# The head of a two-block transformer kernel: the first two modulations on VectorE instead of TensorE, three chunks taken along step by step instead of two

## The chip, the cores and the metric

The kernel runs on one core of a Trainium2 chip, as one launch. The metric is the device time of that core in microseconds (us), lower is better. The median of three runs of the kernel before is 1721.9 us (1711.86 to 1724.2).

## The reference

256 tokens of width 1024 go through two blocks in fp32. The first block mixes a gated linear recurrence and a stick-breaking attention and has a gated feed-forward part; the second has two attentions and a mixture of 32 experts. The change touches the first lines of the first block alone:

```python
mod = c @ ada_w[l] + ada_b[l]                       # c: 1 x 1024, ada_w: 1024 x 6144
sh1, sc1, gt1, sh2, sc2, gt2 = [m[:, None, :] for m in jnp.split(mod, 6, axis=-1)]
h = rmsnorm(x, norm1_g[l]) * (1.0 + sc1) + sh1      # x: 256 x 1024
p = h @ w_in[l]                                     # w_in: 1024 x 7168
xr, yr, q, k, v, ga, gb = jnp.split(p, cuts, axis=-1)
...
q = head_rmsnorm(q.reshape(b_, s_, ATT_HEADS, HEAD_DIM), q_norm_g[l])
k = head_rmsnorm(k.reshape(b_, s_, ATT_HEADS, HEAD_DIM), k_norm_g[l])
```

## The kernel before, in words

Activations lie transposed: `xT` and `hT` are 128 partitions x 8 blocks x 256 tokens, where block k holds the features 128k to 128k+127. Each engine has a program written out by hand, and the order in it is the order of the code; the engines wait for one another through counting semaphores. Weights come as pieces of 1 MB through a ring of 17 slots (`ring`). One list, `plan`, sets the order of the pieces; SyncE issues them in that order, and from the 18th on it waits until the piece that lay in the slot has been used. After the plan's pieces the 384 pieces of the experts' weights go through the same ring.

The head of the program works so. ScalarE squares `xT` in four pieces (L1190). VectorE adds the four to one (L1635, L1637), and TensorE sums the 128 partitions with a matrix of ones in one matmul of 256 columns (L529). ScalarE takes the root (L1172), VectorE the reciprocal (L1596), and eight multiplications (L1652) make `hT` out of `xT`. The shift sh1 and the scale sc1 come block by block: a piece `("ada", 0, n)` holds the 2 x 128 columns of `ada_w` for block n. TensorE multiplies it by c in eight narrow matmuls (`shift_and_scale`, L537), ScalarE copies four partial rows out of PSUM (L1202), TensorE sums and turns them (`shift_and_scale_turn`, L548), VectorE adds the bias and makes the gain (L1657, L1659), and ScalarE applies both to block n of `hT` (L1206). As soon as block k of `hT` is there, `first_chunks` (L561) adds its share to the first two chunks of q, ("qk", 0) and ("qk", 1): four matmuls of 256 columns per k, into banks 0 and 1. A chunk is 256 columns of `w_in`, 16 matmuls in all. These three kinds of work alternate on TensorE, one after the other, for n = 0 to 9.

Behind this each of the six other q and k chunks runs in one go (L515), with one matmul of 512 columns for a head norm between two chunks (`qk_norm`, L592). That needs VectorE's copy of the chunk (L1687) and ScalarE's square of it (L1214). The root (L1220), a reciprocal of 512 elements (L1692) and two scalings follow. VectorE also evaluates a softplus of `rg_lambda` in some 30 operations on 128 x 8, most of them between the steps of the head (L1640 to L1677), the rest after it.

The later modulations are summed on VectorE already: c lies broadcast over the partitions in `cb`, the weights are transposed, and two multiplications with an accumulating output (L1617) make 2 x 128 values of one piece.

Of the kernel before, what the change touches and what calls it, by code (L numbers as in the profile page):

```python
# [15 lines left out]
S = 256  # L16
# [17 lines left out]
def _layout_cols():  # L34
    n = 0
    for name, w in (("e4", 1), ("c", 8), ("ada_b", 48), ("b_ada2", 48), ("norm1", 8), ("norm2", 8),
                    ("conv_w", 32), ("conv_b", 8), ("ba", 8), ("bx", 8), ("lam", 8), ("qg", 1), ("kg", 1),
                    ("fw", 144), ("fb", 48), ("pre_mix", 8), ("post_mix", 8), ("pre_ffn", 8),
                    ("post_ffn", 8), ("gq", 2), ("gkv", 1)):
        COLS[name] = (n, w)  # L40
        n += w
    return n
# [63 lines left out]
piece_done ada_row ada_tr cb ada_use mod  # L106
qk_raw qk_sq qk_sum qk_rt qk
pad xp_cp xc vv gel
att_qk att_ln att_l1 att_cum att_lg att_p att_o att_y
# [32 lines left out]
class Board:  # L142
# [35 lines left out]
    def lay_scratch(self):  # L178
# [17 lines left out]
        self.lt = [carve(8) for _ in range(6)]  # L196
        self.sq1 = [carve(512) for _ in range(4)]
        self.rst1 = carve(256)
        self.rows = carve(512)
# [76 lines left out]
    def lay_pieces(self):  # L276
# [15 lines left out]
        ada(0, range(3, 8))  # L292
        for n in range(2, 8):
            w_in(("qk", n), (8, 12)[n // 4] + n % 4)
# [41 lines left out]
        ada0 = [("ada", 0, k) for k in range(8)]  # L336
        for key in ada0 + [key for key, _, _ in plan if key not in ada0]:
            if key[0] not in ("b1", "ada") or key[:2] == ("ada", 0):
# [88 lines left out]
def sync_program(e, K):  # L427
# [4 lines left out]
    for i, (key, src, n) in enumerate(K.plan):  # L432
        if i >= RING:
# [66 lines left out]
def tensor_program(e, K):  # L500
# [29 lines left out]
    def shift_and_scale(n):  # L530

        v = landed(("ada", 0, n))
        if n >= 2:
            e.wait_ge(S.ada_row, n - 1)
        for k in range(8):
            g = 32 * (k % 4)
            ins = mm(B[5 + n % 2][g:g + 32, 0:256], K.C("c", k).to_broadcast([128, 32]), v[:, 256 * k:256 * k + 256],  # L537
                     start=(k < 4), stop=(k >= 4), skip_group_check=True)
        ins.then_inc(S.piece_done, 1)

    def shift_and_scale_turn(n):

        e.wait_ge(S.ada_row, n + 1)
        if n >= 2:
            e.wait_ge(S.hn, n - 1)
        for m in range(2):
            o = 256 * (n % 2) + 128 * m
            ins = mm(B[3 + n % 2][:, m:m + 1], K.rows[:, o:o + 128], K.C("e4"), start=True, stop=True,  # L548
                     skip_group_check=True)
        ins.then_inc(S.ada_tr, 1)  # L550

    def first_chunks(k):

        for c in range(2):
            v, b = K.piece(("qk", c)), K.main_bank(("qk", c))
            if k == 0:
                landed(("qk", c))
            if c == 0:
                e.wait_ge(S.h, k + 1)
            for j in range(2):  # L560
                ins = mm(b[:, 256 * j:256 * j + 256], v[:, k * 256 + j * 128:k * 256 + j * 128 + 128], K.hT[:, k, :],  # L561
                         start=(k == 0 and j == 0), stop=(k == 7), skip_group_check=True)
            if k == 7:
                ins.then_inc(S.piece_done, 1)
# [29 lines left out]
    for n in range(8):  # L594
        if n >= 2:
# [308 lines left out]
    e.wait_ge(S.consts, 4)  # L904
# [252 lines left out]
def scalar_program(e, K):  # L1157
    S, B, a, act = K.S, K.bank, K.a, e.activation
# [27 lines left out]
    e.wait_ge(S.consts, 3)  # L1186
# [10 lines left out]
    for n in range(9):  # L1197
        if n < 8:
            landed(("ada", 0, n))
            if n >= 2:  # L1200
                e.wait_ge(S.ada_tr, n - 1)
            act(K.rows[:, 256 * (n % 2):256 * (n % 2) + 256], B[5 + n % 2][:, 0:256], ACT.Copy).then_inc(S.ada_row, 1)  # L1202
        if n:
            k = n - 1
            e.wait_ge(S.hn, k + 1)
            act(K.hT[:, k, :], K.hT[:, k, :], ACT.Identity, bias=K.modc[:, 0, k:k + 1],  # L1206
                scale=K.mc[:, k:k + 1]).then_inc(S.h, 1)
# [377 lines left out]
def vector_program(e, K):  # L1585
# [40 lines left out]

    e.memset(K.eps[:, :], EPS).then_inc(S.consts, 1)
# [3 lines left out]
    for c in range(1, 4):  # L1631
        e.wait_ge(S.sq, c + 1)
        if c > 1:
            e.wait_ge(S.vec, done.n)
        tt_(K.sq1[0], K.sq1[0], K.sq1[c], ALU.add).then_inc(S.vec, done.one())  # L1635
    e.wait_ge(S.vec, done.n)
    tt_(K.sq1[0][:, 0:256], K.sq1[0][:, 0:256], K.sq1[0][:, 256:512], ALU.add).then_inc(S.vec, done.one())  # L1637
    lt = K.lt
    e.wait_ge(S.coef, 1)
    ts_(lt[1], lt[0], 2.0, None, ALU.add).then_inc(S.vec, done.one())  # L1640
    e.wait_ge(S.vec, done.n)
    e.reciprocal(lt[1], lt[1]).then_inc(S.vec, done.one())
    e.wait_ge(S.vec, done.n)
# [846 lines left out]
```

## Time and profile before

| | us |
|---|---|
| median of 3 runs | 1721.9 |
| lowest and highest run | 1711.86, 1724.2 |
| profiled execution, first to last instruction (span) | 1709.3 |
| TensorE busy in it | 1613.8 (94%) |
| VectorE busy | 587.9 (34%) |
| ScalarE busy | 352.9 (21%) |
| head: until the last matmul of the first two chunks | about 43.8 |

Of the profiled execution the span alone is known. The lowest run is 2.6 us above that span. A busy TensorE is not one at its peak, since the ends of pipelined matmuls are modelled. An fp32 matmul shows as two MATMUL records.

### The profile page before, as it was taken

What the parts mean: (1) busy time and instruction counts of PE and PEld (TensorE: products, weight loads), DVE (VectorE), ACT (ScalarE), POOL (GpSimd) and SP (SyncE); (2) the same over time, 40 slices, a digit from 0 to 9 for tenths busy, and PEclk for the clock granted to TensorE, in tenths of its full rate; (3) what the DMA queues carried; (4) which work ended last, traced back from release to release, by engine and by line L of the source; (5) the groups of instructions that cost most, each with busy time, mean ns of one, the idle gap of its engine ahead of it and who ended that gap; (6) DMA issues with size and microseconds to landing.
All of it is one profiled execution on the core that took longest, in us unless ns stands there. A gap on an engine that the chain in (4) does not pass through costs nothing. (4 is left out here: it accounts for less than half of the span.)

```text
span 1709.3 us, 20875 instructions
## 1 busy us (share of the span) xinstructions
PE 1613.8 (94%) x7480; PEld 899.7 (53%) x7480; DVE 587.9 (34%) x1355; ACT 352.9 (21%) x658; POOL 0.2 (0%) x4
## 2 busy tenths in 40 slices
PE   7999989999999898879999998999999899999997
PEld 4888878788888776733333332333333233333332
DVE  3657762789710364232122111112112111212112
ACT  3126552332200134121111111111111110101111
POOL 0000000000000000000000000000000000000000
PEclk9999999999999998988999999999999899999999
DMA  9936675458963330238999999999999999999995
GB/s 396 395 133 246 246 274 183 160 202 324 386 250 120 127 131 1 99 127 361 420 420 420 421 419 420 421 420 420 419 421 420 420 414 405 420 420 420 420 420 224
DMA packets 77221, 545.49 MB, mean 319 GB/s; under 512 B 8944, under 2 KB 9456, under 8 KB 11536
## 3 DMA queue, kind: packets, MB, share of 16 engines
q1 hardware_dynamic: 76048, 542.31, 78.5%
q8 instruction: 94, 1.54, 0.4%
q10 hardware_dynamic: 1024, 1.18, 0.2%
q14 instruction: 55, 0.45, 0.1%
HBM read 542.41 MB, written 1.05 MB: 318 GB/s over the span
## 5 line engine op out<-in xcount | busy, mean ns | idle before, releaser
L1000 PE MATMUL bank<-ring,scr 128*64 128x512 f32 x2048 | 455.5, 600 | 10.5 <-DMA ring<-in_w_mlp 10.5
L515 PE MATMUL bank<-hT,ring 128*128 128x256 f32 x1664 | 369.7, 383 | 7.2 <-ACT hT L1180 7.2
L515 PEld LDWEIGHTS bank<-hT,ring 128*128 128x128 f32 x1664 | 319.6, 193 | 55.4 <-issue 11.6
L1000 PEld LDWEIGHTS bank<-ring,scr 128*64 128x64 f32 x2048 | 145.2, 138 | 303.5 <-issue 267.6
L1033 PE MATMUL bank<-ring,hT 128*64 128x512 f32 x1024 | 233.9, 597 | 1.9 <-DMA ring<-in_w_mlp 1.8
L2273 DVE TENSOR_SCALAR scr<-bank 128x256 f32<-128x256 f32 x64 | 27.0, 422 | 388.3 <-PE bank L1000 388.3
L1033 PEld LDWEIGHTS bank<-ring,hT 128*64 128x64 f32 x1024 | 68.4, 136 | 140.8 <-issue 131.7
L2343 DVE COPY hT<-bank 64x512 f32<-64x512 f32 x32 | 22.2, 694 | 313.4 <-PE bank L1033 283.8
L1500 ACT ACTIVATE scr<-scr 128x256 f32<-128x256 f32 x64 | 26.7, 417 | 494.8 <-DVE scr L2273 494.8
L1617 DVE SCALAR_TENSOR_TENSOR ring<-ring,cb 128x1024 f32<-128x1024 f32 x80 | 94.5, 1219 | 0.0
L713 PE MATMUL bank<-scr,ring 128*128 128x256 f32 x384 | 83.5, 379 | 1.6 <-ACT scr L1343 1.6
L713 PEld LDWEIGHTS bank<-scr,ring 128*128 128x128 f32 x384 | 72.9, 190 | 11.9 <-ACT scr L1343 2.0
L927 PE MATMUL bank<-scr 128*64 128x512 f32 x272 | 67.6, 620 | 7.2 <-DVE scr L2243 4.6
L1534 ACT ACTIVATE hT<-bank 128x512 f32<-128x512 f32 x32 | 19.1, 598 | 221.3 <-PE bank L943 221.3
L1071 PE MATMUL bank<-hT,scr 128*128 128x512 f32 x128 | 59.2, 605 | 0.8 <-ACT hT L1550 0.8
L927 PEld LDWEIGHTS bank<-scr 128*64 128x64 f32 x272 | 19.5, 142 | 46.5 <-issue 38.0
L1071 PEld LDWEIGHTS bank<-hT,scr 128*128 128x128 f32 x128 | 23.0, 189 | 37.1 <-issue 35.4
L943 PEld LDWEIGHTS bank<-con,scr 128*128 128x128 f32 x136 | 14.9, 146 | 35.0 <-issue 26.5
L2231 DVE COPY scr<-bank 64x256 f32<-64x256 f32 x64 | 27.0, 422 | 13.0 <-PE bank L933 11.7
L1946 DVE SCALAR_TENSOR_TENSOR scr<-scr,col 128x256 f32<-128x256 f32 x48 | 23.1, 481 | 20.5 <-ACT scr L1343 20.2
L1692 DVE RECIPROCAL scr<-scr 128x512 f32<-128x512 f32 x8 | 26.8, 3352 | 9.6 <-ACT scr L1220 9.6
L1986 DVE SCALAR_TENSOR_TENSOR xT<-bank,modc,xT 128x256 f32<-128x256 f32 x8 | 3.5, 479 | 77.4 <-PE bank L713 77.4
(394 smaller groups left out, 1391.7 us busy)
## 6 DMA issues: line engine op xcount, KB each, us to landing
ring<-in_w_mlp SPq DMA_DIRECT2D x384, 1024.0 KB, 23.2
ring<-in_w_in SPq DMA_DIRECT2D x28, 1024.0 KB, 14.8
ring<-in_up SPq DMA_DIRECT2D x24, 1024.0 KB, 7.0
ring<-in_w_ada SPq DMA_DIRECT2D x24, 1024.0 KB, 6.9
ring<-in_ada_w SPq DMA_DIRECT2D x16, 1024.0 KB, 4.9
ring<-in_down SPq DMA_DIRECT2D x12, 1024.0 KB, 14.9
ring<-in_ada SPq DMA_DIRECT2D x8, 1024.0 KB, 18.6
ring<-in_w2in SPq DMA_DIRECT2D x6, 1024.0 KB, 9.8
```

The source lines that it names most:

```text
L515: ins = mm(b[:, 256 * j:256 * j + 256], v[:, k * 256 + j * 128:k * 256 + j * 128 + 128], rhs[:, k, :], start=(k == 0), stop=(k == 7))
L713: ins = mm(b[j][:, 0:256], v[:, k * 256 + j * 128:k * 256 + j * 128 + 128], K.ff[:, kk * 8 + k, :], start=(kk == 0 and k == 0), stop=(kk = ...
L927: ins = mm(B[3][64 * hf:64 * hf + 64, :], K.sel[c][:, tt, :], K.h4[:, tt, hf * 512:(hf + 1) * 512], start=(tt == 0), stop=(tt == 1), skip_ ...
L1000: ins = mm(HID[0][n][64 * hf:64 * hf + 64, :], K.xe[0][x % 2][:, xo:xo + 64], v[:, o0:o0 + 512], start=False, stop=(k == 7), skip_group_ch ...
L1033: ins = mm((K.down_bank(x), B[1])[c][g:g + 64, :], K.aT[c][x % 2][:, 128 * q + 64 * hf:128 * q + 64 * hf + 64], v[:, j * 1024 + oh * 512:j ...
L1071: ins = mm(OUT[tt][oh][:, :], K.pairT[p % 2][oh][:, tt * 128:(tt + 1) * 128], K.ypair[oh], start=False, stop=False, skip_group_check=True)
L1500: act(K.w2[:, sl], K.actb[0][:, sl], ACT.Sigmoid, scale=1.702).then_inc(S.m_sig, 1)
L1617: ins = stt(w, w, 1.0, K.cb[:, :], ALU.mult, ALU.mult, accum_out=K.modc[:, n // 3, m:m + 1])
L1692: e.reciprocal(rst, rst).then_inc(S.vec, done.one())
L1946: stt(w[:, m, :], u[:, m, 1:257], C("fw", 48 + n), w[:, m, :], ALU.mult, ALU.add).then_inc(S.vec, done.one())
L2231: ins = e.tensor_copy(K.pairT[x // 2 % 2][g ^ x % 2][rows, :], B[3][rows, 0:256])
L2273: ts_(w[:, sl], gate, 7.0, None, ALU.min).then_inc(S.m_glu, 1)
```

## The change

The pieces `("ada", 0, n)` hold transposed weights now. VectorE multiplies each half by the broadcast c and sums along it (`first_modulation`), 2 operations of 1024 elements per block. c comes as one row of 4 KB; TensorE spreads it over the partitions with two matmuls of 512 columns, and VectorE copies the result to `cb`; a load of 512 KB goes. ScalarE makes shift and gain from the sums with two tiny operations per block. TensorE's narrow matmuls and turns and ScalarE's row copies are gone. TensorE sums the squares itself, in eight matmuls of 256 columns instead of three and a half additions on VectorE and one matmul. Three chunks go along step by step. The softplus moves behind the q and k chunks 3 to 6.

```diff
-        ada(0, range(3, 8))
-        for n in range(2, 8):
+        ada(0, [3])
+        w_in(("qk", 2), 10)
+        ada(0, range(4, 8))
+        for n in range(3, 8):
             w_in(("qk", n), (8, 12)[n // 4] + n % 4)
...
+            elif before[0] == "ada":
+                e.wait_ge(S.ada_sum, 2 * before[2] + 2)
...
         if key == ("ada", 0, 7):
-            e.dma_start(K.cb[:, :], a["cb"]).then_inc(S.ld_cb, 16)
             e.dma_start(K.con[:, 256:NCONST], a["consts"][:, 256:NCONST]).then_inc(S.ld_con2, 16)
...
+    e.wait_ge(S.ld_cb, 16)
+    e.wait_ge(S.consts, 1)
+    for n in range(2):
+        ins = mm(B[5 + n][:, :], K.one_row, K.c_row[:, 512 * n:512 * n + 512], start=True, stop=True)
+    ins.then_inc(S.c_mm, 1)
     e.wait_ge(S.ld_col, 32)
-    e.wait_ge(S.vec, 4)
-    mm(B[7][:, 0:256], ones, K.sq1[0][:, 0:256], start=True, stop=True).then_inc(S.nsum, 4)
...
-    for n in range(10):
-        if n < 8:
-            shift_and_scale(n)
-        if 1 <= n < 9:
-            shift_and_scale_turn(n - 1)
-        if n >= 2:
-            first_chunks(n - 2)
+    for c in range(4):
+        norm_sum(0, c, K.sq1[c])
...
+    def first_step(c, k):
+
+        v, b = K.piece(("qk", c)), K.main_bank(("qk", c))
+        for j in range(2):
+            ins = mm(b[:, 256 * j:256 * j + 256], v[:, k * 256 + j * 128:k * 256 + j * 128 + 128], K.hT[:, k, :],
+                     start=(k == 0 and j == 0), stop=(k == 7), skip_group_check=True)
+        if k == 7:
+            ins.then_inc(S.piece_done, 1)
...
     for n in range(8):
-        if n >= 2:
+        if n >= 3:
             chunk(("qk", n))
         if n:
             qk_norm(n - 1)
...
+    e.dma_start(K.c_row, a["c_row"]).then_inc(S.ld_cb, 16)
     e.dma_start(K.con[:, 0:256], a["consts"][:, 0:256]).then_inc(S.ld_col, 16)
     e.dma_start(K.col[:, :], a["cols"]).then_inc(S.ld_col, 16)
...
-    for n in range(9):
-        if n < 8:
-            landed(("ada", 0, n))
-            if n >= 2:
-                e.wait_ge(S.ada_tr, n - 1)
-            act(K.rows[:, 256 * (n % 2):256 * (n % 2) + 256], B[5 + n % 2][:, 0:256], ACT.Copy).then_inc(S.ada_row, 1)
...
+    e.wait_ge(S.gain, 1)
+    for k in range(8):
+        e.wait_ge(S.ada_sum, 2 * k + 1)
+        act(K.mc[:, 8 + k:9 + k], K.modc[:, 0, k:k + 1], ACT.Identity, bias=C("ada_b", k)).then_inc(S.act, done.one())
+        e.wait_ge(S.ada_sum, 2 * k + 2)
+        act(K.mc[:, k:k + 1], K.modc[:, 0, 8 + k:9 + k], ACT.Identity, bias=K.mc[:, 16 + k:17 + k],
+            scale=C("norm1", k)).then_inc(S.act, done.one())
+        e.wait_ge(S.hn, k + 1)
+        e.wait_ge(S.act, done.n)
+        act(K.hT[:, k, :], K.hT[:, k, :], ACT.Identity, bias=K.mc[:, 8 + k:9 + k],
+            scale=K.mc[:, k:k + 1]).then_inc(S.h, 1)
...
+    def first_modulation(k):
+
+        i = K.at[("ada", 0, k)]
+        v = K.piece(("ada", 0, k))
+        e.wait_ge(S.ring[i % RING], 16 * (i // RING + 1))
+        for j in range(2):
+            m, w = 8 * j + k, v[:, 1024 * j:1024 * j + 1024]
+            ins = stt(w, w, 1.0, K.cb[:, :], ALU.mult, ALU.mult, accum_out=K.modc[:, 0, m:m + 1])
+            ins.then_inc(S.ada_sum, 1)
...
+        if n == 4:
+            softplus_first()
+        elif 4 < n < 7:
+            softplus_terms(4 * n - 20, 4 * n - 16)
+        elif n == 7:
+            softplus_last()
```

On TensorE the steps of the head stood like this before. L537 is the product with c of one piece, L548 the turn, L561 the first two chunks, L592 the norm of a head; w0, w1, ... are the slots' semaphores.

```order
L529 MATMUL bank7<-scr,con 128x256 [waits vec,ld_col]
L537 MATMUL bank5<-ring,col 32x256 [waits w0]
...
L561 MATMUL bank0<-hT,ring 128x256 [waits h,w2]
L561 MATMUL bank0<-hT,ring 128x256
L561 MATMUL bank1<-hT,ring 128x256 [waits w4]
L561 MATMUL bank1<-hT,ring 128x256
L537 MATMUL bank6<-ring,col 32x256 [waits ada_row,w5]
L537 MATMUL bank6<-ring,col 32x256 x7
L548 MATMUL bank3<-col,scr 128x1 [waits hn,ada_row]
```

Now it is the following, where L532 spreads c, L525 and L526 sum the squares and L542 is a step of a chunk.

```order
L532 MATMUL bank5<-scr 128x512 [waits consts,ld_cb]
L532 MATMUL bank6<-scr 128x512
L525 MATMUL bank7<-scr,con 128x256 [waits sq,ld_col]
L526 MATMUL bank7<-scr,con 128x256
...
L542 MATMUL bank0<-hT,ring 128x256 [waits h,w2]
...
L542 MATMUL bank1<-hT,ring 128x256 [waits w4]
L542 MATMUL bank1<-hT,ring 128x256 x3
...
L542 MATMUL bank2<-hT,ring 128x256 [waits w6]
L542 MATMUL bank2<-hT,ring 128x256 x7
...
L542 MATMUL bank2<-hT,ring 128x256 x2
L584 MATMUL bank<-scr,con 128x512 [waits qk_sq,ld_con2]
L584 MATMUL bank<-scr,con 128x512 [waits qk_sq]
```

Between two waits for `h` nothing but chunk matmuls is left; the third chunk catches up on k = 0 to 3 in a row of eight, and the norms of the first two heads' chunks stand behind one another.

On VectorE the head reads so now. L1627 fills `cb`, L1629 makes a term of the gains, L1638 is `first_modulation`, L1589 the reciprocal, L1643 the scaled blocks, L1695 the copy of a chunk.

```order
L1627 COPY cb<-bank5 128x512 [waits c_mm]
L1629 SCALAR_TENSOR_TENSOR mc<-col 128x8 [waits ld_col]
L1638 SCALAR_TENSOR_TENSOR ring,modc<-ring,cb 128x1024 [waits w0,vec]
L1638 SCALAR_TENSOR_TENSOR ring,modc<-ring,cb 128x1024
L1589 RECIPROCAL scr<-scr 128x256 [waits norm_rt]
L1643 TENSOR_TENSOR hT<-xT,scr 128x256 [waits rstd]
L1643 TENSOR_TENSOR hT<-xT,scr 128x256 x3
L1638 SCALAR_TENSOR_TENSOR ring,modc<-ring,cb 128x1024 [waits w1]
...
L1643 TENSOR_TENSOR hT<-xT,scr 128x256 x4
L1638 SCALAR_TENSOR_TENSOR ring,modc<-ring,cb 128x1024 [waits w3]
...
L1695 COPY scr<-bank0 128x512 [waits h,piece_done,ld_con2]
```

The eight pairs of products are one after another on VectorE, with the reciprocal and the eight scaled blocks between the first three of them.

## Rows read from the trace of the kernel before

**Rows 1.** The page: span, and TensorE and DMA in 40 equal slices.
```profile
span 1709.3 us, 20875 instructions
...
PE   7999989999999898879999998999999899999997
...
DMA  9936675458963330238999999999999999999995
```

**Rows 2.** Stretches: length, busy PE, PEld, DVE, ACT, POOL, granted clock, DMA share, GB/s.
```profile
12.00:14.00 2.00, 2.00 (x24) 0.96 (x20) 1.97 (x2) 0.38 (x1) 0.00 (x0) 1.00 1.01 422
...
42.70:85.50 42.80, 41.92 (x183) 34.35 (x182) 27.04 (x21) 7.78 (x13) 0.00 (x0) 1.00 0.97 395
...
811.90:854.60 42.70, 42.70 (x196) 14.46 (x192) 8.36 (x23) 4.54 (x9) 0.00 (x0) 1.00 1.01 420
```

**Rows 3.** The chain that ended last, two of its pieces: start, us, what.
```profile
1663.84 26.43 DMA ring<-in_w_mlp
1690.32 1.96 PE bank L1033 x8
```

**Rows 4.** What TensorE waited for after 43 us: total, times, longest.
```profile
PE bank L1000 <- DMA ring<-in_w_mlp: 10.5, 18, 1.3
PE bank L614 <- DVE scr L1735: 7.5, 4, 4.7
PE bank L515 <- ACT hT L1180: 7.2, 2, 3.6
```

**Rows 5.** Timeline of the head: start, us, engine, line, operation [idle before].
```profile
6.07 2.19 ACT L1190 ACTIVATE scr<-xT 128x512 f32<-128x512 f32 x4 [2.90 <-DMA xT<-in_xT]
...
9.30 0.21 ACT L1192 ACTIVATE scr<-col 128x8 f32<-128x8 f32 x1 [1.05 <-DMA col<-in_cols]
...
10.14 1.19 PE L529 MATMUL bank<-scr,con 128*128 128x256 f32 x2 [10.14 <-DVE scr L1640]
...
11.37 0.48 ACT L1172 ACTIVATE scr<-bank,eps 128x256 f32<-128x256 f32 x1
...
11.88 1.75 DVE L1596 RECIPROCAL scr<-scr 128x256 f32<-128x256 f32 x1 [0.96 <-ACT scr L1172]
...
13.67 2.77 DVE L1652 TENSOR_TENSOR hT<-xT,scr 128x256 f32<-128x256 f32 x8
...
16.63 1.93 PE L537 MATMUL bank<-ring,col 128*32 128x256 f32 x16 [0.78 <-DMA ring<-in_ada]
16.74 0.60 ACT L1206 ACTIVATE hT<-hT,modc,mc 128x256 f32<-128x256 f32 x1 [1.38 <-DVE mc L1659]
...
19.37 3.67 PE L561 MATMUL bank<-hT,ring 128*128 128x256 f32 x8
...
24.43 1.97 PE L561 MATMUL bank<-hT,ring 128*128 128x256 f32 x8
...
33.08 1.07 PE L537 MATMUL bank<-ring,col 128*32 128x256 f32 x16
...
34.08 0.61 PE L548 MATMUL bank<-col,scr 128*128 128x1 f32 x4
...
36.45 1.07 PE L537 MATMUL bank<-ring,col 128*32 128x256 f32 x16
```

**Rows 6.** Timeline behind the head: the norm of a head's chunk and full chunks.
```profile
43.17 1.35 DVE L1687 COPY scr<-bank 128x512 f32<-128x512 f32 x2 [1.32 <-PE bank L561]
...
43.90 1.29 ACT L1214 ACTIVATE scr<-scr 128x512 f32<-128x512 f32 x2 [2.64 <-DVE scr L1687]
...
44.67 1.10 PE L592 MATMUL bank<-scr,con 128*128 128x512 f32 x2 [0.88 <-ACT scr L1214]
...
45.60 7.07 PE L515 MATMUL bank<-hT,ring 128*128 128x256 f32 x32
...
52.51 1.02 PE L592 MATMUL bank<-scr,con 128*128 128x512 f32 x2
...
53.37 7.07 PE L515 MATMUL bank<-hT,ring 128*128 128x256 f32 x32
```

**Rows 7.** Timeline of VectorE: two sums of a later modulation; a k chunk.
```profile
126.80 1.22 DVE L1617 SCALAR_TENSOR_TENSOR ring<-ring,cb 128x1024 f32<-128x1024 f32 x1
...
127.94 1.22 DVE L1617 SCALAR_TENSOR_TENSOR ring<-ring,cb 128x1024 f32<-128x1024 f32 x1
...
83.77 0.69 DVE L1687 COPY scr<-bank 128x512 f32<-128x512 f32 x1 [1.60 <-PE bank L515]
```

**Rows 8.** Small operations of the head: groups by line, busy us, mean ns.
```profile
L1665 DVE TENSOR_SCALAR scr<-scr 128x8 f32<-128x8 f32 x8 | 1.4, 171 | 0.3
```

**Rows 9.** DMA issues: count, KB, us from issue to landing.
```profile
con<-in_consts ACTq DMA_DIRECT2D x1, 128.0 KB, 5.5
...
scr<-in_posc ACTq DMA_DIRECT2D x1, 1.0 KB, 1.8
```

More of the change, by code:

```diff
@@ L194, in carve_top @@
             return self.scr[:, place[1]:place[1] + n]
-        self.lt = [carve(8) for _ in range(6)]
+        self.lt = [self.modc[:, 1, 8 * n:8 * n + 8] for n in range(5)]
         self.sq1 = [carve(512) for _ in range(4)]
         self.rst1 = carve(256)
-        self.rows = carve(512)
+        self.c_row, self.one_row = carve(1024)[0:1], carve(128)[0:1]
         place[0] = 0
@@ L335, in lay_pieces @@
         self.done_at, n = {}, 0
-        ada0 = [("ada", 0, k) for k in range(8)]
-        for key in ada0 + [key for key, _, _ in plan if key not in ada0]:
-            if key[0] not in ("b1", "ada") or key[:2] == ("ada", 0):
+        for key, _, _ in plan:
+            if key[0] not in ("b1", "ada"):
                 n += 1
@@ L541, in shift_and_scale_turn @@
-    def shift_and_scale_turn(n):
-        e.wait_ge(S.ada_row, n + 1)
-        if n >= 2:
[L545 to L564, printed above, removed]
@@ L573, in tensor_program @@
+    landed(("qk", 0))
+    for k in range(2):
+        e.wait_ge(S.h, k + 1)
+        first_step(0, k)
+    landed(("qk", 1))
+    for k in range(2):
+        first_step(1, k)
+    for k in range(2, 4):
+        e.wait_ge(S.h, k + 1)
+        first_step(0, k)
+        first_step(1, k)
+    landed(("qk", 2))
+    for k in range(4):
+        first_step(2, k)
+    for k in range(4, 8):
+        e.wait_ge(S.h, k + 1)
+        for c in range(3):
+            first_step(c, k)
     e.wait_ge(S.ld_con2, 16)
@@ L1641, in vector_program @@
-    e.wait_ge(S.vec, done.n)
-    e.reciprocal(lt[1], lt[1]).then_inc(S.vec, done.one())
-    e.wait_ge(S.vec, done.n)
-    tt_(lt[1], lt[1], lt[0], ALU.mult).then_inc(S.vec, done.one())
-    e.wait_ge(S.vec, done.n)
-    tt_(lt[2], lt[1], lt[1], ALU.mult).then_inc(S.vec, done.one())
-    e.wait_ge(S.vec, done.n)
-    ts_(lt[3], lt[2], 1.0 / 19.0, 1.0 / 17.0, ALU.mult, ALU.add).then_inc(S.vec, done.one())
+    e.wait_ge(S.c_mm, 1)
+    for n in range(2):
+        e.tensor_copy(K.cb[:, 512 * n:512 * n + 512], B[5 + n][:, :]).then_inc(S.vec, done.one())
@@ L1649, in vector_program, with first_scaled @@
+    def first_scaled(k0, k1):
+        for k in range(k0, k1):
+            tt_(K.hT[:, k, :], K.xT[:, k, :], K.rst1, ALU.mult).then_inc(S.hn, 1)
+    e.wait_ge(S.vec, done.n)
+    first_modulation(0)
     norm_end(0, K.rst1)
     e.wait_ge(S.rstd, 1)
-    for k in range(8):
-        tt_(K.hT[:, k, :], K.xT[:, k, :], K.rst1, ALU.mult)
-    for n in range(8):
-        e.wait_ge(S.ada_tr, n + 1)
-        both = K.modc[:, 0, 0:16].rearrange("p (j b) -> p b j", j=2)[:, n, :]
-        bias = C("ada_b", 0, 16).rearrange("p (j b) -> p b j", j=2)[:, n, :]
-        tt_(both, B[3 + n % 2][:, 0:2], bias, ALU.add).then_inc(S.vec, done.one())
+    first_scaled(0, 4)
@@ L1658, in vector_program, with softplus_first @@
+    first_modulation(1)
+    first_scaled(4, 8)
+    for k in range(2, 8):
+        first_modulation(k)
+    e.sem_inc(S.mod, 1)
+    e.wait_ge(S.ld_con2, 16)
+    lt = K.lt
+    def softplus_first():
+        e.wait_ge(S.coef, 1)
+        ts_(lt[1], lt[0], 2.0, None, ALU.add).then_inc(S.vec, done.one())
         e.wait_ge(S.vec, done.n)
-        stt(K.mc[:, n:n + 1], K.modc[:, 0, 8 + n:9 + n], 1.0, C("norm1", n), ALU.add, ALU.mult).then_inc(S.hn, 1)
-        m = 15 - 2 * n
+        e.reciprocal(lt[1], lt[1]).then_inc(S.vec, done.one())
@@ new lines, in softplus_first, with softplus_terms, softplus_last @@
+        e.wait_ge(S.vec, done.n)
+        ts_(lt[3], lt[2], 1.0 / 19.0, 1.0 / 17.0, ALU.mult, ALU.add).then_inc(S.vec, done.one())
+    def softplus_terms(n0, n1):
+        for n in range(n0, n1):
+            e.wait_ge(S.vec, done.n)
+            tt_(lt[3], lt[3], lt[2], ALU.mult).then_inc(S.vec, done.one())
+            e.wait_ge(S.vec, done.n)
+            ts_(lt[3], lt[3], 1.0 / (15 - 2 * n), None, ALU.add).then_inc(S.vec, done.one())
+    def softplus_last():
+        e.wait_ge(S.vec, done.n)
+        stt(lt[3], lt[3], 2.0, lt[1], ALU.mult, ALU.mult).then_inc(S.vec, done.one())
+        ts_(lt[4], C("lam", 0, 8), -1.0, 0.0, ALU.mult, ALU.max).then_inc(S.vec, done.one())
+        e.wait_ge(S.vec, done.n)
+        tt_(lt[3], lt[3], lt[4], ALU.add).then_inc(S.vec, done.one())
+        e.wait_ge(S.vec, done.n)
+        ts_(K.sp8[:, 0:8], lt[3], 8.0, None, ALU.mult)
+        ts_(K.sp8[:, 8:16], lt[3], -8.0, None, ALU.mult)
+        ts_(K.hb[:, 0:8], C("ba", 0, 8), 0.5, None, ALU.mult)
+        ts_(K.hb[:, 8:16], C("bx", 0, 8), 0.5, None, ALU.mult).then_inc(S.gatec, 1)
```

67 lines of the change are left out of this document (15 added, 52 removed).

## The prediction

> **What bounds the kernel now.** I read the slices first, then stretches, then the end of the chain, then the timeline of the head. TensorE is busy nearly all along, and from the 20th slice to the last but one the DMA engines are full [rows 1]. In that stretch they move 420 GB/s beside a TensorE that is shown busy all the time [rows 2], and the chain's last long piece is 26.43 us of expert weights, with one piece's matmuls behind it [rows 3]. So the second half is paced by the stream of expert weights. That stream is no reason why a gain at the head should be lost: its slots are freed by TensorE's use of earlier pieces, so it starts earlier when TensorE gets there earlier. Nowhere in the kernel does an engine wait for a time, only for another engine. Between the head and the experts TensorE leads: its longest waits after the head are for VectorE and ScalarE, each some us in total [rows 4], and these engines wait for TensorE in turn. So what is won or lost until the head's end should reach the end of the kernel nearly whole.
>
> The question is then when TensorE starts the fourth q/k chunk, ("qk", 3). That is 53.37 us before [rows 6], behind the two chunks that go along, the norm of the first, the third chunk, and the norm of the second. In the head TensorE never rests: from 23 us a period is 3.37 us (36.45 - 33.08), which is product, turn and four chunk matmuls in line [rows 5]. Half of it is chunk work.
>
> **TensorE's clock.** The same eight records of L561 take 3.67 us at 19.37 us and 1.97 us at 24.43 us [rows 5]: the 1.2 and the 2.4 GHz level. The granted clock reads 1.00 even at 12 us [rows 2], so in this head the durations tell the level, not that column. TensorE had worked from 10.14 us on with narrow matmuls mostly and got to the higher level at about 23 us, when the first four full-width chunk matmuls were through. Per matmul of 256 columns I take 7.07 / 16 = 0.442 us at the higher level [rows 6] and at the lower (3.67 - 0.2) / 4 = 0.87 us [rows 5], where 0.2 is the tail that four of them show at the higher one, 1.97 - 4 x 0.442.
>
> **The change, part by part.**
> *c.* The row of c is 4 KB. Nothing of this size is loaded in the head; the nearest rows are 1.8 us for 1 KB in a quiet queue and 5.5 us for 128 KB beside the first loads [rows 9]. Issued at 0.74 us, it lands between 2.5 and 6.2 us; I take 3.5, near the small one. Two matmuls of 512 columns at the lower level are four of 256: 3.5 us, until 7.0 (6.0 to 9.7). Two copies of 0.68 us each [rows 6] end at 8.4 (7.4 to 11.1). The constants land at 9.3 us [rows 5], and 0.45 us later now behind one more issue, so VectorE starts its first products at about 9.9 (to 11.3) and ends them by 12.3 (to 13.7). The norm is not there before 17 us, so all of this is covered, by 3 us at the least. The Trainium skill, page "DMA: Bandwidth & Descriptors", section "Anatomy of one DMA — SWDGE (gpsimd) path", gives about 2 us of fixed cost per transfer; that would put the landing near 2.8 us, and the sum would not move.
>
> *The norm.* Before, one matmul at 10.14 us. Now eight, from 9.75 us on. At the lower level 8 x 0.87 = 7.0 us: end, with the tail's first tenth, at 16.85; at the higher level 3.5 us: 13.3. I take the lower, since before TensorE was at that level until 23 us. Root 0.48, reciprocal 1.75 [rows 5]: until 19.15, 5.5 us later than the 13.63 of before. Then blocks of 0.34 us: four until 20.55.
>
> *VectorE's sums.* Two per block, spaced 127.94 - 126.80 = 1.14 us [rows 7], so 2.3 us a block. The second block's: 20.55 to 22.85. Four more scaled blocks: 24.25. Six more pairs: 26.55, 28.85, and so on to 38.05. ScalarE adds 0.05 + 0.2 + 0.05 + 0.6 = 0.9 us, from a 0.21 us small operation and 0.60 us for a block [rows 5]. So block k of hT is ready at 20.2, 23.8, 27.5, 29.8, 32.1, 34.4, 36.7 and 39.0 us. The pieces are there: the fourth landed at 16.6 us [rows 5], and 1 MB at 422 GB/s [rows 2] is 2.5 us; in the new order the pieces for blocks 3 to 7 come sixth and eighth to eleventh, at 21.6, 26.6, 29.1, 31.6 and 34.1 us, each 2 us or more ahead of its sum.
>
> *TensorE's chunks.* The two matmuls of k = 0 run at 20.2. From 23.8 us 46 matmuls are left. I let the lower level hold for 3.6 us more (as long as the four of before took): 4.1 matmuls. The other 41.9 take 18.5 us: end at 45.9 us. Are blocks late in this? c0 and c1 reach k = 2 at 28.2 (ready 27.5), k = 3 at 30.0 (29.8); the third chunk's eight run until 35.3; then k = 4 to 7 start at 35.3, 38.0, 40.6, 43.3, all behind their blocks. So TensorE paces, not VectorE, and the end is 45.9.
>
> *Norms of the heads.* Chunk 0 is done 1.8 us before that; copy and square need 0.7 + 0.65 [rows 6], so its norm runs right at 45.9. Chunk 1 is done at 45.0; its square is ready at 46.5, and its norm follows the first. Two norms take 2 x 0.87. ("qk", 3) starts at 47.65 us, against 53.37: **5.7 us** earlier.
>
> *Softplus.* Some 30 small operations go to VectorE behind chunks 4 to 7. One is 0.17 us [rows 8], about 0.2 with its wait, so at most 8 x 0.2 = 1.6 us per chunk. VectorE idles 1.6 us there per k chunk [rows 7], and TensorE needs a copy only a chunk later: nothing. Without that cover it would be 1.6 us twice. What it frees in the head was idle time of VectorE. The 512 KB load that goes was not waited for.
>
> **Sum.** 1709.3 - 5.7 = 1703.6 us of span. As the lowest run is 2.6 us above the span shown and the median 12.6 above, I put the same difference on the median: 1721.9 - 5.7 = **1716.2 us**, -0.33%. Gain at the ends of the unknowns: without any lower level after 23.8 us, 1.8 more, 7.5; with the higher level from the norm on, blocks come 3.5 us earlier or, the last, when its piece allows (34.1 + 2.3 + 0.9 = 37.3 us), the third chunk has caught up at 31.6, and 31.6 + 4 x 2.65 = 42.2 is 3.7 earlier than 45.9: 9.4.
>
> **Rivals.**
> *The clock stays low (slower).* TensorE now rests from 16.85 to 20.2 and from 21.9 to 23.8 us, where before it did not. If the higher level does not come while it waits block by block, the 46 matmuls take 46 x 0.87 = 40.0 us, the end is 63.8, and ("qk", 3) starts at 65.6: 12.2 us slower, 1734.1. It decides at the point where the lower level has lasted 3.6 + 2 x 5.7 = 15 us, to 38.8 us. Against it: at the lower level four matmuls need 3.5 us and blocks come every 2.3, so TensorE has no gap at all from 23.8 us on, and before the level rose with just such work [rows 5]. The Trainium skill, page "TensorE: Matmul & The Clock Gate", section "What's actually happening", says that "the default state is throttled, and activity releases the throttle", and its section "HAM oscillation — how this bites in real kernels" that waits between short bursts of matmuls bring the low level back. By that rule the norm's matmuls buy nothing for the chunks, as in my sum; the trace of before agrees with the first sentence, and has no such gap to show the second.
> *VectorE paces.* If a sum takes longer beside 420 GB/s of writes than the 1.14 us of a quieter stretch, the last block is late. TensorE's last step is 2.65 us, so the last block has until 43.3 us: 4.3 us of slack over the 14 sums behind the norm, 0.31 us each. At 1.7 us a sum it would be 39.0 + 14 x 0.56 = 46.8, end 49.5, and the gain 2: 1720.
> *Won and lost again.* The 5.7 us turn into waits of TensorE for VectorE or ScalarE in the attention, whose chains are as long as before [rows 4]. VectorE's end of the q/k part is softplus plus copies later relative to TensorE. No change: 1721. Against it: in the q/k part both engines wait for TensorE [rows 6, 7].
> *More than said.* The higher level comes early: gain 7.5 to 9.4, 1712.5 to 1714.4.
>
> **How the numbers follow.** The forecast (gain 4 to 7.5) has 0.55, more than said 0.12, VectorE's pace 0.08, won and lost again 0.15, the low clock 0.10, of which most is a partial one. All of these lie within 1% of 1721.9, which is 17.2 us and about what a measurement of this kernel can tell from no change. The whole spread of cases, 1712.5 to 1734, is less wide than that. What may carry a result over the line is the spread of runs: 12.3 us between three of the same kernel. A median of the changed kernel that falls on the lowest run's side is 1711.9 - 5.7 = 1706; on the other side 1724.2 - 2 = 1722. I take 1704 to 1724. Faster by over 1%: 0.07; within 1%: 0.91; slower by over 1%: 0.02.
>
> **What would show it.** The first chunk matmuls of k = 1 near 24 us and TensorE without gaps behind them; the last of chunk 2 at about 46; L584 twice in a row; the first matmul of ("qk", 3) near 47.7 us; pairs of L1638 every 2.3 us without a wait for the ring from 24 to 38 us; the reciprocal L1589 near 17.4 us; the experts' full DMA stretch some 6 us earlier, at the same 420 GB/s. I am wrong if TensorE waits for h behind 30 us, if L542 stays at 0.87 us per matmul, if the row of c lands after 9 us, or if the stretch between ("qk", 3) and the experts gets longer.

## The result and the profile after

The changed kernel takes 1724.06 us (median of 20 runs, 1721.74 to 1725.87), the kernel before 1712.9 us (20 runs, 1710.97 to 1724.54). The ratio on record is 1.0039, 95% interval 1.0025 to 1.0053 (the two medians alone would give 1.0065): slower, where 0.33% faster was forecast, and just outside the range of 1704 to 1724.

One thing has to be known to read this. The runs of the kernel before lie in two groups, 13 of the 20 from 1710.97 to 1713.49 and 7 from 1720.6 to 1724.54. All 20 of the changed kernel lie in one group, at the height of the upper one. The forecast had started from three runs, two of which were from the upper group. The share varies: beside the experiments below, the kernel before had 18 of 35, 18 of 29 and 9 of 10 runs in its upper group. So the changed kernel is compared here with each group, and not only with a median that can fall in either.

The page after: span, TensorE, granted clock and DMA in 40 slices. Below it stands the clock's row of the kernel before.

```profile
span 1721.4 us, 20604 instructions
...
PE   6999989999999899879999998999999899999997
...
PEclk8999999999999996878999999999999899999999
DMA  9936675458963330218999999999999999999995
```

```profile
PEclk9999999999999998988999999999999899999999
```

Against [rows 1] the span is 12.1 us longer, though TensorE has less to do in the head. The two clock rows show where to look: apart from the first slice they differ in slices 16 to 18 alone (6, 8, 7 for 8, 9, 8), which is 645 to 775 us.

The head, in order of time (start, us, engine, line, operation, idle before):

```profile
2.40 3.78 PE L532 MATMUL bank<-scr 1*128 1x512 f32 x4 [2.40 <-DMA scr<-in_c_row]
...
12.16 1.22 PE L525 MATMUL bank<-scr,con 128*128 128x256 f32 x2 [5.98 <-DMA col<-in_cols]
...
14.03 1.06 PE L525 MATMUL bank<-scr,con 128*128 128x256 f32 x2
...
18.09 0.59 PE L526 MATMUL bank<-scr,con 128*128 128x256 f32 x2
...
19.23 1.75 DVE L1589 RECIPROCAL scr<-scr 128x256 f32<-128x256 f32 x1 [4.61 <-ACT scr L1164]
...
22.22 2.04 PE L542 MATMUL bank<-hT,ring 128*128 128x256 f32 x4 [3.54 <-ACT hT L1199]
...
25.90 22.88 PE L542 MATMUL bank<-hT,ring 128*128 128x256 f32 x92 [1.64 <-ACT hT L1199]
...
39.86 0.39 ACT L1195 ACTIVATE mc<-modc,mc,col 128x1 f32<-128x1 f32 x1 [0.85 <-DVE ring L1638]
...
47.15 1.49 DVE L1695 COPY scr<-bank 128x512 f32<-128x512 f32 x2 [7.33 <-PE bank L542]
...
48.65 1.95 PE L584 MATMUL bank<-scr,con 128*128 128x512 f32 x4
...
50.44 5.78 PE L517 MATMUL bank<-hT,ring 128*128 128x256 f32 x26
```

From 25.90 us on TensorE runs its 46 chunk matmuls (92 records) without a gap and is through at 48.78. ScalarE makes the gain of the last block (L1195) at about 40 us, so TensorE paces, as forecast. The row of c is in use at 2.40 us. The constants, though, come at 12.16 us instead of the 9.75 of the forecast. ("qk", 3) starts at 50.44 us, 2.93 us before the 53.37 of [rows 6].

What follows is the changed kernel, TensorE and VectorE around the last two head norms, between which the kernel before idles 0.59 us:

```profile
88.41 1.02 PE L584 MATMUL bank<-scr,con 128*128 128x512 f32 x2
...
90.74 0.17 DVE L1676 TENSOR_SCALAR modc<-modc 128x8 f32<-128x8 f32 x1
90.82 0.68 DVE L1695 COPY scr<-bank 128x512 f32<-128x512 f32 x1
...
92.22 1.39 PE L584 MATMUL bank<-scr,con 128*128 128x512 f32 x2 [2.79 <-ACT scr L1207]
...
93.41 8.53 PE L517 MATMUL bank<-hT,ring 128*128 128x256 f32 x32
```

VectorE copies the last k chunk 2.2 us after TensorE has moved on (eight softplus operations end at 90.9), TensorE then idles 2.79 us, and the next chunk, ("conv", 0), takes 8.53 us instead of 7.07, with the granted clock at 0.51 from 93.0 to 96.4 us. The chunk behind it, ("v", 0), starts at 101.78 us against 100.81: the head's gain is gone, and 0.97 us more.

These are single traces, and the moment at which the clock rises in the head moves them by about a microsecond. The traces of e4 and e6, which have the head of the kernel before, reach ("v", 0) at 99.60 and 99.51 us; those of e5 and e8, which have the changed one, at 99.72 and 100.68. On the mean of three traces each, the changed kernel gains 3.1 us until ("qk", 3) and is 0.8 us behind at ("v", 0).

Between 101 and 630 us the two traces run side by side; the changed one falls from 0.97 to 1.71 us behind (the same ScalarE operations in both, counted from the end). Then, in the attention of the second block, the stretches of both, with TensorE's granted clock after the five engines (0.50 is the level of 1.2 GHz, 1.00 that of 2.4). First the kernel before:

```profile
644.00:674.70 30.70, 25.22 (x171) 19.03 (x169) 16.38 (x45) 15.50 (x57) 0.00 (x0) 1.00 0.01 2
674.80:685.00 10.20, 8.13 (x30) 7.04 (x31) 2.05 (x4) 3.52 (x6) 0.00 (x0) 0.50 0.00 0
633.80:644.00 10.20, 9.79 (x38) 8.54 (x39) 4.86 (x18) 5.04 (x21) 0.00 (x0) 0.50 0.00 0
```

and the changed kernel:

```profile
639.10:652.70 13.60, 11.29 (x77) 8.73 (x77) 8.79 (x29) 7.12 (x28) 0.00 (x0) 1.00 0.01 2
652.70:680.00 27.30, 27.30 (x100) 19.78 (x100) 9.15 (x24) 9.59 (x35) 0.00 (x0) 0.50 0.00 1
683.50:697.10 13.60, 11.47 (x41) 9.70 (x42) 2.05 (x4) 3.98 (x7) 0.00 (x0) 0.50 0.00 0
```

Before, the clock is high through all heads but the first few. After, it falls at 652.7 us and stays low for 27.3 us, in which TensorE is shown busy without a gap. One head takes 4.0 us there (657.59 to 661.59 us from L792 to L792); before, two heads in a row take 2.16 and 2.76 us, 2.5 on the mean. At the first few heads it is the kernel before that has the longer low stretch, so the changed one is 0.9 us ahead at 650 us; at 697 us it is 11.5 us behind, where it was 1.7 behind at 630. From there to the end little more is lost (0.6 us), and the experts' stream is as before at 420 GB/s. So of 12.1 us 9.8 come from a stage that the change doesn't touch, 600 us behind it.

What stands ahead of the fall, TensorE in the changed kernel:

```profile
648.94 0.50 PE L803 MATMUL bank<-con,scr 128*128 128x128 f32 x3
651.02 0.32 PE L792 MATMUL bank<-scr 128*128 128x384 bf16 x1 [1.59 <-DVE scr L2105]
...
652.94 0.85 PE L803 MATMUL bank<-con,scr 128*128 128x128 f32 x3
```

It waits 1.59 us for VectorE ahead of head 8. The kernel before has the same gap, of 1.96 us even, at 651.88, and its clock stays up.

### The profile page after: what moved, and what is told of

The parts are those of the page before. It is cut to its first block and busy times, and to the rows that moved or that the text cites. A ratio compares the mean times of both kernels' runs of the same rounds, so it can differ in the third digit from the quotient of the medians.

```text
span 1721.4 us, 20604 instructions
## 1 busy us (share of the span) xinstructions
PE 1622.8 (94%) x7338; PEld 906.2 (53%) x7338; DVE 602.7 (35%) x1371; ACT 354.7 (21%) x666; POOL 0.2 (0%) x4
## 5 line engine op out<-in xcount | busy, mean ns | idle before, releaser
L517 PE MATMUL bank<-hT,ring 128*128 128x256 f32 x1632 | 364.8, 385 | 7.2 <-ACT hT L1172 7.2
L517 PEld LDWEIGHTS bank<-hT,ring 128*128 128x128 f32 x1632 | 314.9, 194 | 55.1 <-issue 11.4
```

## The experiments

Twelve runs: most ask which step lost the head's gain and why the clock falls, and e9 and e10 take back two parts of the change. "Theory A" and "rival B" are those of the expectation printed above each result. "The low stretch" is the 27.3 us at the lower clock.

### e1: the softplus right behind the first sums

```diff
+    softplus_first()
+    softplus_terms(0, 8)
+    softplus_last()
...
         if n:
             qk_scale(n - 1)
-        if n == 4:
-            softplus_first()
-        elif 4 < n < 7:
-            softplus_terms(4 * n - 20, 4 * n - 16)
-        elif n == 7:
-            softplus_last()
```

> The changed kernel with its softplus (some 30 small VectorE operations) moved from behind the q/k chunks 4 to 7 to right behind the last sum of the first modulations, where VectorE idles from 39.8 to 47.2 us. Reading of the two traces: between 88 and 101 us the changed kernel loses 3.9 us, because VectorE copies chunk 7 only 2.2 us after its end (eight softplus operations stand before the copy), TensorE waits 2.8 us, and then works 3.4 us at the lower clock. Theory A (softplus is the cause): no wait of more than 1 us at the last two head norms and no low level there, (v, 0) starts near 97.9 us instead of 101.8. Rival B (VectorE is behind anyway, from the reciprocals that start late after three chunks): a wait of 1.5 us or more stays. For the whole: if the 12 us lost between 640 and 700 us, where TensorE's clock is at the lower level for 41 us instead of 20, come from where the work then stands in time against the clock's switching, they may go or stay: 1710 or 1720; if from something the change does in that stage, they stay: 1720.

1718.56 us (12 runs, one at 1704.08, the others from 1716.61 to 1720.2). TensorE around the last norms:

```profile
86.08 1.02 PE L584 MATMUL bank<-scr,con 128*128 128x512 f32 x2
87.69 1.12 PE L584 MATMUL bank<-scr,con 128*128 128x512 f32 x2 [0.59 <-ACT scr L1207]
88.65 7.07 PE L517 MATMUL bank<-hT,ring 128*128 128x256 f32 x32
95.56 5.77 PE L634 MATMUL bank<-ring,hT 128*128 128x256 f32 x26
```

The gap is 0.59 us again and the chunk takes 7.07 us: theory A. From ("qk", 3) at 48.12 us to ("v", 0) at 95.56 it is 47.44 us, as in the kernel before (100.81 - 53.37) and 3.90 less than in the changed one. All fourteen traces agree on this: it is 51.33 to 51.35 us in the four with the softplus late (the changed kernel, e2, e5, e8) and 47.44 or 47.45 in the other ten. That ("qk", 3) comes 2.3 us earlier than in the changed kernel is no effect of the edit, which touches nothing ahead of it: the constants came 0.3 us earlier and the clock rose at 14.9 instead of 17.9 us. The low stretch stayed (646.4 to 673.7 us), and with it most of the loss. One of its twelve runs was 12.5 us below the next.

### e2: the row of c first on SyncE's queue

```diff
+    e.dma_start(K.c_row, a["c_row"]).then_inc(S.ld_cb, 16)
     e.dma_start(K.xT[:, :, :], a["xT"]).then_inc(S.ld_x, 16)
...
-    e.dma_start(K.c_row, a["c_row"]).then_inc(S.ld_cb, 16)
     e.dma_start(K.con[:, 0:256], a["consts"][:, 0:256]).then_inc(S.ld_col, 16)
```

> The changed kernel with one load moved: the row of c is the first transfer of SyncE, and ScalarE's queue begins with the constants, as in the kernel before. Theory A (the constants land at 12.14 us instead of 9.30 because they are issued 0.5 us later and fall behind the first 1 MB pieces): they land at 9.3 to 9.8 again, the norm's matmuls start there, and (qk, 3) starts 2 to 2.8 us earlier than 50.44. Rival B (the row's own transfer is in their way, or the ring's pieces are, wherever the row is issued): they land at about 12 us still, and nothing moves. In the whole 2 us, unless the clock's pattern between 640 and 700 us changes.

1720.08 us (12 runs, 1717.94 to 1720.94). The loads, changed kernel and then e2 (KB, us to landing):

```profile
col<-in_cols ACTq DMA_DIRECT2D x1, 206.5 KB, 10.4
con<-in_consts ACTq DMA_DIRECT2D x1, 128.0 KB, 7.7
```

```profile
col<-in_cols ACTq DMA_DIRECT2D x1, 206.5 KB, 6.1
con<-in_consts ACTq DMA_DIRECT2D x1, 128.0 KB, 2.2
```

Theory A, and more than it expected: the norm's matmuls begin at 7.28 us instead of 12.16, and ("qk", 3) at 43.70 instead of 50.44. Not all of these 6.7 us are the constants'. They give 4.9; the rest is mostly a clock that rose earlier, during the norm, which took 5.3 us for 6.5 (e12, with the same order of loads, has its constants at 7.59 us and ("qk", 3) at 45.61).

The edit moves two things: the constants are issued 0.56 us earlier (0.74 for 1.30 us), and SyncE's large loads begin 0.4 us later (1.16 for 0.74). The kernel before has the first without the second, and its 128 KB take 5.5 us [rows 9]. So both count, and that the large loads stand in the constants' way is the nearest reading; no run moved them alone. The softplus is in its old place here, and its wait comes as well: 9.67 us ahead at ("qk", 3), 5.76 ahead at ("v", 0), again 3.9 lost. The low stretch stayed too (648.8 to 676.1).

### e3: both

> Both: softplus right behind the first sums and the row of c first on SyncE. If both theories hold, (qk, 3) starts at about 48 us, (v, 0) at about 95.5, 5 us before the kernel before (100.8), and the time is 1707 to 1708 where the clock goes as in the kernel before between 640 and 700 us, and 1718 where it stays low as in the changed kernel.

1713.7 us (12 runs: five from 1699.71 to 1704.62, seven from 1713.4 to 1715.4). ("qk", 3) starts at 45.90 us in the profiled run, which is one of the seven and has the low stretch (644.8 to 672.1). Two groups 10 us apart, as in the kernel before, each about 4 us below what was expected of it; ("qk", 3) was expected at 48 us.

### e4 and e8: more work far from the stage

```diff
         if j >= 4:
             e.wait_ge(S.ff_cp, j - 3)
+        if j == 8:
+            for _ in range(4):
+                mm(B[0][:, 0:256], v[:, 0:128], K.hT[:, 0, :], start=True, stop=True)
         tiles2(v, K.hT, B[j % 4], 8 if j == 0 else None).then_inc(S.piece_done, 1)
```

In e4 this stands in the kernel before, in e8 in the changed one.

> The kernel before with nothing of the change, and four extra matmuls of 256 columns (1.77 us at the higher clock) ahead of the feed-forward chunk 8, near 370 us, where TensorE is busy without a gap. Their output is overwritten. In the changed kernel the same stage runs 1.7 us later than in the kernel before. Theory A (what happens to the clock between 640 and 700 us depends on when the second block's short bursts arrive, measured against the fixed steps at which the clock switches): the time changes by clearly more than 1.8 us, up to 12, or the share of runs near 1722 changes, and the trace shows another pattern of levels after 560 us than that of the kernel before. Rival B (the change itself alters that stage, by another order or by a busier engine): plus 1.8 us and no more, with the same pattern.

> The changed kernel with four extra matmuls (1.77 us) ahead of the feed-forward chunk 8 near 370 us, as e4 did with the kernel before, far from the stage where the clock falls. Theory A (only the moment at which the second block's bursts arrive decides): the pattern of levels between 640 and 700 us changes in most runs, and the time falls by up to 9 us in spite of more work. Rival B (the changed kernel falls into the low stretch at any moment): 1724 + 1.8 = 1726.

The kernel before with 1.77 us more work: all 12 runs from 1711.13 to 1713.95, median 1712.02, the upper group gone (18 of the 35 runs of the kernel before beside it were in that group). The changed kernel with the same: all 12 from 1711.59 to 1715.4, median 1713.9, 10.2 us less than without. The stretch of e8, which answers to the second row of the changed kernel above:

```profile
641.20:675.10 33.90, 28.50 (x193) 21.49 (x192) 18.81 (x54) 17.85 (x67) 0.00 (x0) 1.00 0.01 1
```

Theory A both times. Nothing in the stage was altered, only the moment at which its bursts arrive, and the clock stays up. It also rules out that the change as such must bring the fall about.

### e5 and e6: the gap filled

```diff
         if n == 8:
+            for _ in range(4):
+                mm(b[:, 0:256], ident, K.con[:, 0:256], start=True, stop=True, skip_group_check=True)
             e.wait_ge(S.cs, 3)
```

e5 is the changed kernel with this, e6 the kernel before.

> The changed kernel with four extra matmuls of 256 columns (1.77 us at the higher clock), issued ahead of the wait for the scores of head 8 of the second block's attention. There TensorE idled 1.59 us (at 651 us), and 1.7 us after the end of that gap its clock fell and stayed low for 27.3 us. Their output is overwritten. Theory A (this gap lets the clock fall, and the short matmuls of the eight heads behind it don't bring it up again): the low stretch of 27 us is gone, and the time falls by 9 to 12 us, to 1712 to 1715. Rival B (the fall comes from the load of the stage as a whole, or from TensorE's history): the stretch stays, 1724.

> The same four matmuls in the kernel before. Its runs lie in two groups, about 1712 and 1722. Theory A (the upper group is the same fall of the clock): all runs in one group near 1710 to 1713. Rival B (the groups have another cause): both groups stay.

e5: 1713.39 us (12 runs, 1711.43 to 1715.35), 10.7 less. e6: 1712.12 us (12 runs, 1705.98 to 1713.43): no upper group. The gap and the clock in e5:

```profile
649.33 1.89 PE L792 MATMUL bank<-con 128*128 128x256 f32 x8
651.17 0.34 PE L794 MATMUL bank<-scr 128*128 128x384 bf16 x1
```

```profile
643.30:673.90 30.60, 26.72 (x178) 20.36 (x177) 16.29 (x45) 15.48 (x57) 0.00 (x0) 1.00 0.01 2
```

Theory A. The four matmuls take the place of the wait, so they cost nothing that shows, and the fall doesn't come. Could it be that they only shift the moment, as in e4 and e8? Against this, seven kernels have the filler (e5, e6, e7, e9 to e12), they reach the stage at moments up to 8.7 us apart, and none of their 47 runs stands 10 us above the others of its kernel. The same edit removes the upper group of the kernel before, so that group is taken to be the same fall. No run of that group was profiled, but each run's mean granted clock is on record: beside e5 and e6 it is 0.972 to 0.975 in the lower group and 0.960 to 0.971 in the upper. A stretch of 27.3 us at half the clock is worth 0.008 of a span.

What the filler doesn't explain is why the clock stays up with the wait unfilled in the kernel before, e4 and e8 (1.96, 1.61 and 1.74 us). With the wait the fall came at some moments and not at others, without it in no run; how the two are linked stays open.

Between e5 and e6, which both lack the long low stretch, the change costs 1.3 us. That is near the 0.8 us of the three traces each at ("v", 0): 3.1 gained in the head, 3.9 lost at the last norms. But medians of 12 runs that spread over 4 and 7 us don't settle a difference of this size: the traces of e5 and the kernel before move between 0.3 and 5.0 us against each other in the experts' part alone.

### e7 and e12: e3 with the gap filled

> The kernel of e3 (softplus right behind the first sums, the row of c first on SyncE) with the same four matmuls. Theory A: one group of runs near 1700 to 1704, the lower group of e3, so the head's gain reaches the end: 8 to 11 us below the lower group of the kernel before. Rival B: the upper group of e3 stays, near 1714.

> The kernel of e7 again, on the same chip as e9 to e11, as their base: 1700 to 1704.

1703.82 us (6 runs, 1699.99 to 1704.43; ratio to the kernel before 0.9908, interval 0.9883 to 0.9933) and 1704.93 us (4 runs, 1699.14 to 1705.74). Against e6, the kernel before with the same filler, they take 8.3 and 7.2 us less. This is the version that beats both kernels. ("qk", 3) starts at 45.77 and 45.61 us, and ("v", 0) at 93.21 and 93.06.

### e9, e10, e11: parts undone, against e12 on the same chip

e9 puts the sum of squares back on VectorE:

```diff
-    for c in range(4):
-        norm_sum(0, c, K.sq1[c])
+    e.wait_ge(S.vec, 6)
+    mm(B[7][:, 0:256], ones, K.sq1[0][:, 0:256], start=True, stop=True).then_inc(S.nsum, 4)
...
+    for c in range(1, 4):
+        e.wait_ge(S.sq, c + 1)
+        if c > 1:
+            e.wait_ge(S.vec, done.n)
+        tt_(K.sq1[0], K.sq1[0], K.sq1[c], ALU.add).then_inc(S.vec, done.one())
+    e.wait_ge(S.vec, done.n)
+    tt_(K.sq1[0][:, 0:256], K.sq1[0][:, 0:256], K.sq1[0][:, 256:512], ALU.add).then_inc(S.vec, done.one())
```

> The kernel of e7 with one part of the change undone: VectorE adds the four pieces of squares again and TensorE sums them in one matmul. Theory A (the norm on TensorE is a cost, 8 matmuls at the lower clock for one): the reciprocal starts 2 to 3 us earlier than 14.7 us, and (qk, 3) up to 3 us earlier, unless the pieces of the modulation weights or TensorE's own work then set the pace. Rival B (the norm's matmuls warm the clock and without them the level rises later): (qk, 3) at the same time or later than in e7. In the whole 1700 to 1704.

1704.11 us (4 runs, 1702.84 to 1705.46) against 1704.93: no difference. The first chunk matmuls come 1.5 us earlier than in e12 (16.02 for 17.52 us), and ("qk", 3) 0.7 earlier (44.90). The chunks end 1.8 us earlier (19.71 + 22.52 = 42.23 for 21.20 + 22.81 = 44.01), so theory A has the right sign in the head, though the reciprocal comes 1.5 us earlier (13.04 for 14.52) and not 2 to 3, and rival B falls. But then TensorE idles 0.88 us for the first chunk's square: VectorE's softplus, right behind the sums, ends at 41.7 us, and its copy waits for that. In this order the norm on TensorE buys nothing and costs nothing that a run shows; what it costs in another order was not tried.

e10 takes two chunks along instead of three (`first_step` for c = 0 and 1 at each k, the piece of the third behind all modulation pieces, `chunk` from n = 2 on).

> The kernel of e7 with another part undone: two chunks go along with the first modulations, and the third follows in one go, its weights after all modulation pieces as before. Theory A (VectorE's sums take 2.3 us per block, two chunks' steps 1.77, so TensorE idles about 0.5 us per block and the third chunk's 7.1 us come behind): (qk, 3) 2 to 4 us later than in e7, 1706 to 1707. Rival B (TensorE at the lower clock has no room for the third chunk anyway): no difference.

1709.94 us (5 runs, 1708.88 to 1711.46): 5.0 us more than e12. Its head:

```profile
31.41 1.99 PE L541 MATMUL bank<-hT,ring 128*128 128x256 f32 x8 [0.30 <-ACT hT L1190]
33.70 1.99 PE L541 MATMUL bank<-hT,ring 128*128 128x256 f32 x8 [0.30 <-ACT hT L1190]
35.99 1.99 PE L541 MATMUL bank<-hT,ring 128*128 128x256 f32 x8 [0.30 <-ACT hT L1190]
41.32 1.10 PE L574 MATMUL bank<-scr,con 128*128 128x512 f32 x2 [3.34 <-ACT scr L1198]
42.26 7.07 PE L516 MATMUL bank<-hT,ring 128*128 128x256 f32 x32
```

A period is 2.29 us, VectorE's two sums, and four matmuls don't fill it; then TensorE waits 3.34 us for copy and square, of which the copy starts at 39.83 us only, right behind the softplus, where the chunks' last matmul ended at 37.98. So, as an estimate, some 2 of the 5.0 us belong to the softplus's place (39.83 - 37.98) and the other 3 to the third chunk; no run parts them.

e11 is e1 with the gap filled.

> The kernel of e1 (softplus right behind the first sums, the row of c still first on ScalarE's queue) with the four extra matmuls ahead of head 8. Against e5, which differs in the softplus alone: 3 to 4 us less, 1709 to 1710. Against e7, which differs in the row of c alone: 4 us more. If the softplus cost nothing, 1713 as e5.

1707.97 us (4 runs, 1705.62 to 1709.33). Against e12 the row of c is worth 3.0 us (3.6 in the traces at ("v", 0)), against e5, on another chip, the softplus 5.4, where the two traces show 3.9 of it at the norms. The rest lies within the 3.7 us over which the four runs spread.

One thing is left over. In the stage behind the attention, from about 705 to 765 us, the clock is low for 20.5 us in all in the traces of the kernel before, the changed one, e3 and e4, and for 27.3 us in the other ten, which lose 1.8 to 2.7 us there against the kernel before. All seven kernels with the filler are among the ten. So the filler protects one stage and not the next, and no run was made on that.

## Why the prediction was wrong

The span was forecast 5.7 us shorter and came out 12.1 longer. The 17.8 us between them add up so, by the two traces: 2.8 in the head until ("qk", 3), 3.9 at the last head norms, 0.7 up to 630 us, 9.8 in the second block's attention, 0.6 behind it.

**The bound, and what passes through.** Right for TensorE between head and experts and for the experts' stream, which ran at 420 GB/s as before. Wrong was "what is won or lost until the head's end should reach the end of the kernel nearly whole". I had taken every step behind the head as of fixed length. The heads of the second block are not: their length depends on the clock's level, and the level on the moment at which they arrive. e4 and e8 show it with 1.77 us of work, e5 and e6 with the gap. This is the step that failed most: 9.8 of the 12.1 us by which the span grew, where the forecast had nothing.

**The start of the sum.** I put the difference on the median of three runs, 1721.9. Two of the three were of the upper group, which I took for spread. A gap of 10 us between runs of one kernel was a row of the result to be explained, not a width for the range. Against the upper group's median the changed kernel is 1.6 us slower, against the lower one's 11.8. That the median came out only 7.9 us above the 1716.2 of the forecast, where the span missed by 17.8, is luck: a start that was 9.0 too high hid half of the miss.

**"Softplus ... nothing".** Wrong, -3.9 us (e1). I had compared 1.6 us of work with 1.6 us of idle time and not asked whether that idle time would be there. After three chunks at once VectorE starts its reciprocals late against TensorE and is 6.3 us behind at the third chunk's copy, which starts at 55.11 us though the chunk was through at 48.78. In the kernel before the same copy follows at once, at 52.71 us for 52.67. First the changed kernel, then the kernel before:

```profile
55.11 0.68 DVE L1695 COPY scr<-bank 128x512 f32<-128x512 f32 x1
```

```profile
52.71 0.69 DVE L1687 COPY scr<-bank 128x512 f32<-128x512 f32 x1 [1.50 <-PE bank L515]
```

VectorE used just that idle time to catch up: at the next two copies it is 4.2 and 2.9 us behind. The operations took it away, and the last chunk found it still behind. "TensorE needs a copy only a chunk later" fails at the last chunk, where two norms stand behind one another.

**The row of c and the constants.** The row came at 2.40 us, just ahead of the near end of my bounds and 1.66 us after its issue, and was covered as said. The 2 us that the forecast takes from the Trainium skill, page "DMA: Bandwidth & Descriptors", section "Anatomy of one DMA — SWDGE (gpsimd) path", would have made it 2.8; that section is on loads that GpSimd issues, and this one stood in ScalarE's queue. "0.45 us later now behind one more issue" was the step that failed: 2.8 us later than before in fact (12.14 for 9.30). The likeliest reason is that the first large loads get in ahead (e2). Worth 3.0 us (e11 against e12).

**The clock in the head.** I gave the lower level 3.6 us from 23.8 on; it held until 31.5 us (5.6 us of the gapless stretch) in this run, until 28.6 in e1's. The end of the chunks came at 48.8 for 45.9: the stretch began 2.1 us late (25.9 for 23.8), because of the constants, and took 0.8 us more (22.9 for 22.1), because of the clock. The norm's matmuls did bring the level up, at 17.9 us, and it fell again at 21.3, when TensorE had been waiting since 18.7. That TensorE then ran without a gap and paced the head was right, and so were 2.3 us per pair of sums and 1.7 us for two norms (1.79). ScalarE took 1.1 us for 0.9, which TensorE waited for at the first two blocks alone.

**The rivals.** None was what happened as a whole. "The clock stays low" had the right quantity in the wrong place, and for another reason: it let TensorE wait block by block, and in the low stretch TensorE waits for nobody. The Trainium skill, page "TensorE: Matmul & The Clock Gate", section "HAM oscillation — how this bites in real kernels", describes waits between short bursts of matmuls that bring the low level back. The trace agrees in part: the level fell 1.7 us after a wait of 1.59 us, shorter than the waits described there, and with that wait filled it did not fall (e5). That it then stayed low for 27.3 us while TensorE is shown busy throughout is not what the section describes. "Won and lost again" (0.15) named the attention's chains and also "softplus plus copies later", and set both aside because "both engines wait for TensorE" in the q/k part. The second is what happened at the last norms, 3.9 us, and the reason against it was the one that failed.

## What to carry to other kernels

Look at the granted clock of every stage, not only of the one that is changed: a stage of short matmuls with gaps can cost 10 us more or less when anything upstream moves, and a few filler matmuls in a gap in which TensorE waits anyway held it up here at no cost that showed. When runs of one kernel fall in two groups, find out why before a small change is judged. Idle time of an engine that is catching up is not free cover, and the place of a small load among large ones can be worth several times its issue (0.5 us of issue, 3.0 us of kernel).

## What the runs showed of the hardware

- 27.3 us at the lower level with TensorE shown busy in all of it (27.30 of 27.30 us; the ends of matmuls are modelled, so very short gaps could hide), the same length in the changed kernel, e1, e2 and e3: being shown busy was not enough to bring the level back. The matmuls there have 64 to 384 columns. Why the level stayed low is not shown.
- 1.77 us of additional work made a kernel 10.2 us faster (e8), and 1.77 us of filler 10.7 us (e5).
- In the head the granted clock reads 1.00 until the first switch that the trace has, while the same matmul (a pair of records) takes 1.06 us at 14.03 us and 0.59 at 18.09. The durations are to be trusted there.
- A load of 128 KB on ScalarE's queue took 2.1 to 2.3 us to land where SyncE's first large load was issued 0.4 us after it (six traces), 5.5 or 5.6 us where the two were issued together (three traces), and 7.4 to 7.7 us where it was issued 0.56 us behind that load (five traces).
